# A pair loop of expert blocks in which part of the up split goes to GpSimd and the sums of halves and rows come first

## The chip, the cores and the metric

The kernel runs on one core of one Trainium2 chip. The metric is the device time of one execution in microseconds, lower being better. Engines: TensorE (PE in the profile), VectorE (DVE), ScalarE (ACT), GpSimd (POOL) and SyncE (SP), which here only starts transfers.

## The reference, cut to what matters

Two transformer blocks on 256 tokens of width 1024, in fp32. The first has three kinds of attention, the second a convolution with sparse attention and then a mixture of experts. Only the experts matter for this change. Each token goes to 8 of 64 experts, each with hidden width 256:

```python
def expert_block(args):
    e, toks, gs = args
    xb = t[toks]
    return swiglu(xb, w1[e], w3[e], w2[e]) * gs[:, None]     # (silu(x @ w1) * (x @ w3)) @ w2
routed = segment_sum(out, row_tok)                            # rows back to their tokens, summed
```

The weights of one expert are 1 MB each for w1, w3 and w2.

## The kernel before

Up to about 650 us the kernel computes the first block and the attention of the second. Then a loop runs over a list of expert blocks; a block is one expert with up to 128 of its tokens. Its length is a run-time value. The blocks alternate. Even ones are "whole": room for 128 tokens. Odd ones are "half": room for 64 tokens. The loop's bodies are written out for BODY = 4 blocks.

Precision comes from splits. Every operand x is held as x_hi = round(x) in a fast fp32 form, written by ScalarE, and x_lo = x - x_hi, written by VectorE. A product is the sum of passes hi*hi, hi*lo and lo*hi. A whole block makes 24 matmuls of 128x512 in its up product (8 steps k, three passes). A half block puts x_hi in the lower 64 columns of the stationary operand and x_lo in the upper 64, makes 16 matmuls, and then adds the two halves of the result ("sum of halves": ScalarE copies the lower half to `hsum`, VectorE adds the other half to it).

The up weights of a block (w1 as m = 0, w3 as m = 1) are split in four pieces of 128x1024, named (kh, m): kh is the half of the steps k (k 0 to 3 or 4 to 7). A matmul of step k reads both m. The down weights are split in two pieces. The up weights of block i + 1 are split while block i is worked on, its down weights in its own body.

The order within block i on each engine is written out by hand; semaphores carry the dependences.

- TensorE (`expert_block`, L2110): up product (L2124) into `hidden_b`; transposes of the rows of block i + 1 into `y_b` (`turn_rows`, L2083 to L2096); the scatter of block i - 1, which adds y into `acc_b` by means of the 0/1 matrix `put` (L2104, in two halves; the second one gives `block_done`); transposes of h (L2144) into `turned_b`; the token search of block i + 2 (`find_tokens`, L2079, into columns of `hidden_b`); the down product (L2162) into `y_b`. In a whole block the second half of the scatter stands behind the transposes of h.
- ScalarE: two roundings of down weights (L1173); two of the four up roundings of block i + 1 (L1156, pieces of kh 0); in a half block the copy of the lower half (L1183); silu (L1189); the rounding of the rows (`round_rows`, L1146 and L1151); h_hi (L1192); the other two up roundings; y_hi (L1200) twice.
- VectorE (`expert_block`, L1695): two subtractions of down weights (L1702); two of up weights (L1676); in a half block the sum of halves (L1708); h = silu * up (L1711); the low part of the rows (`rest_of_rows`, L1664 and L1670); the low part of h (L1715); `take_tokens` (L1656 to L1658), which copies what the token search found; two more up subtractions; y_lo (L1725) twice.
- GpSimd: `make_pick` for block i + 2 (L901, a 0/1 matrix for the token search); after `block_done` of this body the matrix `put` for block i (L931); the indirect transfer `gather_rows` for block i + 2 (L912).
- SyncE: for block i, once down_lo of block i - 2 is made, the transfers of w1, w3 and w2 into the raw buffer that it used, and then small columns for block i + 2.

## Time and profile before

| | us |
|---|---|
| median of 3 runs (1066.08 to 1070.39) | 1069.08 |
| the profiled execution | 1068.22 |
| its span in the trace | 1066.3 |
| TensorE matmuls busy | 980.1 (92%) |
| VectorE busy | 783.9 (74%) |
| ScalarE busy | 584.1 (55%) |
| GpSimd busy | 284.4 (27%) |

Busy times are over the whole span. The expert loop fills roughly the last 400 us, and there the shares differ. Matmuls are pipelined: one takes 0.40 us from start to end, and the next starts 0.23 us after it. "Idle before" in a row is the time in which the engine stood before that instruction, and the arrow names what ended it.

### The profile page before, as it was taken

The page shows a single profiled execution, that of the slowest core. Times are in us where ns is not written, and L with a number is a line of the kernel's source. Part 1 is how long each engine was busy: PE and PEld are TensorE (multiplying, and loading weights), DVE is VectorE, ACT ScalarE, POOL GpSimd, SP SyncE. Part 2 cuts the span into 40 slices and gives each one's busy share as a digit, 9 for nine tenths or more (in the row PEclk, how much of TensorE's full clock was granted, in tenths as well). Part 3 has the DMA queues.
Part 4 walks back from the last instruction along what each step waited for, and adds up shares of the span by engine and source line. Part 5 has one row for each costly group of instructions (what it writes and reads, how often), then busy time and mean ns, then how long its engine had stood idle before and what let it go on. Part 6 is the DMA issues. An engine that isn't in the chain of part 4 may idle for free. (4 is left out here: it accounts for less than half of the span.)

```text
span 1066.3 us, 16044 instructions
## 1 busy us (share of the span) xinstructions
PE 980.1 (92%) x4988; PEld 777.4 (73%) x4988; DVE 783.9 (74%) x1351; ACT 584.1 (55%) x894; POOL 284.4 (27%) x357
## 2 busy tenths in 40 slices
PE   8999999999999999989879989899898989999886
PEld 7877877788766676778768876677676777777664
DVE  4677888678843543567775655889989889898987
ACT  4554565435533242435426424777767777777774
POOL 5154442224100000031226113233222322232221
PEclk9999999999999899999989999999999999999998
DMA  9877767759624243436242317788778877887773
GB/s 308 275 257 256 248 227 252 251 183 309 213 90 150 89 158 119 169 95 234 80 158 80 112 55 267 288 313 318 285 279 317 317 276 271 310 315 290 285 308 143
DMA packets 79285, 238.54 MB, mean 224 GB/s; under 512 B 12732, under 2 KB 18933, under 8 KB 65922
## 3 DMA queue, kind: packets, MB, share of 16 engines
q1 hardware_dynamic: 66002, 196.60, 50.4%
q0 software_dynamic: 12656, 40.87, 11.4%
q8 instruction: 29, 0.48, 0.2%
q10 hardware_dynamic: 576, 0.41, 0.1%
q14 instruction: 22, 0.18, 0.1%
HBM read 235.55 MB, written 2.16 MB: 223 GB/s over the span
## 5 line engine op out<-in xcount | busy, mean ns | idle before, releaser
L1846 PE MATMUL bank<-w_hi,a_hi 128*128 128x512 f32 (+2 forms) x512 | 205.8, 402 | 8.6 <-POOL w_lo L857 3.8
L1846 PE MATMUL bank<-w_hi,a_lo 128*128 128x512 f32 (+2 forms) x512 | 196.8, 384 | 0.0
L1846 PE MATMUL bank<-w_lo,a_hi 128*128 128x512 f32 (+2 forms) x512 | 196.4, 384 | 0.0
L1281 DVE TENSOR_TENSOR w_lo<-ring,w_hi 128x1024 fp32r<-128x1024 f32 (+2 forms) x132 | 152.9, 1181 | 53.2 <-ACT w_hi L991 48.6
L991 ACT ACTIVATE w_hi<-ring 128x1024 fp32r<-128x1024 f32 (+2 forms) x140 | 141.0, 1023 | 73.8 <-PE bank L1846 70.1
L1676 DVE TENSOR_TENSOR up_lo<-raw_weights,up_hi 128x1024 fp32r<-128x1024 f32 x136 | 161.2, 1227 | 1.0 <-ACT up_hi L1156 0.5
L1156 ACT ACTIVATE up_hi<-raw_weights 128x1024 fp32r<-128x1024 f32 x136 | 135.6, 1048 | 1.3 <-DMA raw_weights<-in_w_dram 1.3
L1846 PEld LDWEIGHTS bank<-w_hi,a_hi 128*128 128x128 f32 x512 | 96.5, 188 | 38.4 <-issue 16.6
L1846 PEld LDWEIGHTS bank<-w_hi,a_lo 128*128 128x128 f32 x512 | 96.4, 188 | 19.8
L1846 PEld LDWEIGHTS bank<-w_lo,a_hi 128*128 128x128 f32 x512 | 96.7, 189 | 18.3 <-issue 1.4
L2124 PE MATMUL bank<-up_hi,x_block_hi 128*128 128x512 f32 x264 | 104.4, 395 | 1.0 <-issue 1.0
L2124 PE MATMUL bank<-up_lo,x_block_hi 128*128 128x512 f32 x264 | 104.4, 396 | 0.0
L931 POOL TENSOR_SCALAR put<-slots,block_tokens_f 128x256 fp32r<-128x256 f32 x33 | 30.5, 924 | 233.0 <-issue 233.0
L818 POOL DMA_DIRECT2D merged<-in_w_ada_dram x96 | 53.2, 556 | 127.5 <-DVE ada_acc L1420 93.9
L798 POOL TENSOR_SCALAR mean_squares<-mean_squares 128x8 f32<-128x8 f32 (+2 forms) x32 | 9.9, 310 | 283.9 <-ACT logits L944 204.1
L1702 DVE TENSOR_TENSOR down_lo<-raw_weights,down_hi 128x1024 fp32r<-128x1024 f32 x66 | 77.9, 1222 | 7.5 <-ACT down_hi L1173 7.4
L2162 PE MATMUL bank<-down_hi,h_hi 128*128 128x512 f32 x132 | 58.9, 446 | 18.0 <-DVE h_hi L1715 17.4
L1173 ACT ACTIVATE down_hi<-raw_weights 128x1024 fp32r<-128x1024 f32 x66 | 66.0, 1051 | 0.3 <-issue 0.3
L1420 DVE SCALAR_TENSOR_TENSOR ada_acc<-merged,c_col,ada_acc 128x512 f32<-128x512 f32 x84 | 62.7, 747 | 4.2 <-DMA merged<-in_w_ada_dram 1.0
L1200 ACT ACTIVATE y_hi<-bank,block_gates 128x512 fp32r<-128x512 f32 x66 | 45.4, 689 | 32.8 <-PE bank L2162 32.1
L2124 PEld LDWEIGHTS bank<-up_hi,x_block_hi 128*128 128x128 f32 x264 | 50.0, 189 | 13.2 <-issue 1.2
L2124 PEld LDWEIGHTS bank<-up_lo,x_block_hi 128*128 128x128 f32 x264 | 49.6, 188 | 12.1
(281 smaller groups left out, 1874.3 us busy)
## 6 DMA issues: line engine op xcount, KB each, us to landing
raw_weights<-in_w_dram SPq DMA_DIRECT2D x102, 1024.0 KB, 6.9
ring<-in_w_in_dram SPq DMA_DIRECT2D x58, 1024.0 KB, 5.9
merged<-in_w_ada_dram POOLq DMA_DIRECT2D x96, 256.0 KB, 4.4
ring<-in_w_out_dram SPq DMA_DIRECT2D x8, 1024.0 KB, 5.8
ring<-in_w_branch_dram SPq DMA_DIRECT2D x6, 1024.0 KB, 4.8
bias<-rel_rows SPq DMA_DIRECT2D x40, 128.0 KB, 4.9
ring<-in_ws_dram SPq DMA_DIRECT2D x2, 1024.0 KB, 5.1
merged<-in_x_dram SPq DMA_DIRECT2D x2, 512.0 KB, 5.7
```

The source lines that it names most:

```text
L818: gp.dma_start(ada_row(q), src).then_inc(S(f"ada_loaded_{q % ADA_SLOTS}"), 16)
L991: act.activation(w_parts[0][:, 2 * p:2 * p + 2, 0:w], view(j, kind)[:, 2 * p:2 * p + 2, :], ACT.Copy)\
L1156: act.activation(up_hi[:, r % 2, 4 * kh:4 * kh + 4, m, :], raw_up(raw[:, 1 - r % 2, :], kh, m), ACT.Copy)\
L1173: act.activation(down_hi[:, f, :], raw[:, 1 - r % 2][:, UP + f * DM:UP + (f + 1) * DM], ACT.Copy)\
L1200: act.activation(y_hi[:, hf * CH:(hf + 1) * CH], y_b[hf][:, :], ACT.Copy, scale=gcol[:, r, 0:1])\
L1281: dve.tensor_tensor(w_parts[1][:, 2 * p:2 * p + 2, 0:w], view(JOB[it[1:3]], kind)[:, 2 * p:2 * p + 2, :], w_parts[0][:, 2 * p:2 * p + 2, 0 ...
L1420: dve.scalar_tensor_tensor(out=o, in0=ada_row(q), scalar=c_col[:, 1, k:k + 1], in1=o, op0=ALU.mult, op1=ALU.add) .then_inc(S("ada_step" if ...
L1676: dve.tensor_tensor(up_lo[:, r % 2, 4 * kh:4 * kh + 4, m, :], raw_up(raw[:, 1 - r % 2, :], kh, m), up_hi[:, r % 2, 4 * kh:4 * kh + 4, m, : ...
L1702: dve.tensor_tensor(down_lo[:, f, :], raw[:, 1 - r % 2][:, UP + f * DM:UP + (f + 1) * DM], down_hi[:, f, :].bitcast(F32), ALU.subtract).th ...
L1846: mm = pe.matmul(ps[:, 0:wide], a_parts[za][:, k, t * P:(t + 1) * P], w_parts[zw][:, k, 0:wide], start=start, stop=stop)
L2124: mm = pe.matmul(hidden_b[:, :], (xe_hi, xe_lo)[zx][:, k, :], (up_hi, up_lo)[zw][:, r % 2, k].rearrange("p m n -> p (m n)"), start=(k == 0 ...
L2162: mm = pe.matmul(y_b[hf][:, :], (h_hi, h_lo)[zh][:, f, :], (down_hi, down_lo)[zw][:, f, hf * CH:hf * CH + CH], start=(n == 0), stop=(n == ...
```

## The change

What moves, and where it goes:

- The token search of block i + 2 stands at the head of TensorE's block, before the up product, and writes to four columns of `turned_b` (`found_b`). VectorE copies its result at the head of its own block.
- In a half block ScalarE makes no up roundings before the copy of the lower half; the rows of the next block are rounded between that copy and the silu; all four up roundings stand behind h_hi. VectorE does the sum of halves right after the down subtractions, then one half of the rows, then h, then the other half of the rows, the low part of h, and then three up subtractions.
- In a whole block VectorE does one up subtraction before h and two behind the low part of h; ScalarE's order stays.
- One of the four up subtractions goes to GpSimd: (0, 1) where the next block is half, (1, 1) where it is whole. GpSimd does it last in its block, behind `put`. TensorE waits for it at k = 0 of a half block, at k = 4 of a whole one.
- GpSimd starts the gather of block i + 2 first in its block, and makes the pick of block i + 3 second.
- SyncE loads the up weights of block i once the up split of block i - 2 is done (VectorE's three pieces and GpSimd's one), and the down weights once down_lo of block i - 2 is done.

```diff
@@ sync
-                        sp.wait_ge(S("down_lo"), 2 * i - 2)
-                        load_down(r, load_up(i, r))
+                        sp.wait_ge(S("up_lo"), 3 * i - 3)
+                        sp.wait_ge(S("up_lo_pool"), i - 1)
+                        e = load_up(i, r)
+                        sp.wait_ge(S("down_lo"), 2 * i - 2)
+                        load_down(r, e)
                         load_columns(i + 2, (r + 2) % BODY)
@@ gpsimd
+            def rest_of_up_weights(i, r):
+                kh = 0 if r % 2 else 1
+                gp.wait_ge(S("up_hi"), 4 * i + 2 * kh + 2)
+                gp.sem_inc(S("begun"), 1)
+                gp.tensor_tensor(up_lo[:, r % 2, 4 * kh:4 * kh + 4, 1, :], raw_up(raw[:, 1 - r % 2, :], kh, 1),
+                                 up_hi[:, r % 2, 4 * kh:4 * kh + 4, 1, :].bitcast(F32), ALU.subtract).then_inc(S("up_lo_pool"), 1)
+
             for i in range(2):
                 make_pick(i, i, 1)
                 gather_rows(i, i, 0)
+            make_pick(2, 2, 1)
+            rest_of_up_weights(0, 0)
...
-                        after = (r + 2) % BODY
-                        make_pick(i + 2, after, m4 + 1 + (r + 2) // BODY)
-                        gp.wait_ge(S("slots_loaded"), 16)
+                        gather_rows(i + 2, (r + 2) % BODY, m4 * (BODY // 2) + (r + 2) // 2)
+                        make_pick(i + 3, (r + 3) % BODY, m4 + 1 + (r + 3) // BODY)
                         gp.wait_ge(S("block_done"), i + 1)
                         gp.tensor_scalar(put[:, :], slots[:, S_TOK:S_TOK + TOK], tok_f[:, r, 0:1], None, ALU.is_equal)\
                           .then_inc(S("put_ready"), 1)
-                        gather_rows(i + 2, after, m4 * (BODY // 2) + (r + 2) // 2)
+                        rest_of_up_weights(i + 1, (r + 1) % BODY)
@@ scalar
                         nxt = (r + 1) % BODY
-                        act.wait_ge(S(f"up_loaded_{nxt}"), 32 * (m4 + 1 + (r + 1) // BODY))
-                        for m in range(2):
-                            round_up_weights(nxt, 0, m)
                         if r % 2:
                             act.wait_ge(S("up_done"), i + 1)
                             act.activation(hsum[0:HALF, :], hidden_b[HALF:P, :], ACT.Copy).then_inc(S("half_low_copied"), 1)
+                            round_rows(nxt, m4 * (BODY // 2) + (r + 1) // 2)
                             act.wait_ge(S("half_summed"), m4 * (BODY // 2) + (r // 2 + 1))
+                            act.activation(hs[0:HALF, 0, :], hsum[0:HALF, 0:ED], ACT.Silu).then_inc(S("silu_done"), 1)
                         else:
+                            act.wait_ge(S(f"up_loaded_{nxt}"), 32 * (m4 + 1 + (r + 1) // BODY))
+                            for m in range(2):
+                                round_up_weights(nxt, 0, m)
...
+                        if r % 2:
+                            act.wait_ge(S(f"up_loaded_{nxt}"), 32 * (m4 + 1 + (r + 1) // BODY))
+                            for m in range(2):
+                                round_up_weights(nxt, 0, m)
                         for m in range(2):
                             round_up_weights(nxt, 1, m)
@@ vector
+                take_tokens(i + 2, (r + 2) % BODY, found_b)
                 for f in range(FT):
                     ...down_lo...
-                for m in range(2):
-                    rest_of_up_weights(i + 1, nxt, 0, m)
                 if half:
                     ...sum of halves...
+                    rest_of_whole_rows(pair(1), 0)
+                    ...h...
+                    rest_of_whole_rows(pair(1), 1)
+                    ...low part of h...
+                    for kh, m in UP_OF_EVEN:                      # (0, 0), (0, 1), (1, 0)
+                        rest_of_up_weights(i + 1, nxt, kh, m)
+                else:
+                    rest_of_up_weights(i + 1, nxt, 0, 0)
+                    ...h, rows, low part of h...
+                    for m in range(2):
+                        rest_of_up_weights(i + 1, nxt, 1, m)
@@ tensor
                 pe.wait_ge(S("tokens_ready"), i + 2)
+                find_tokens(i + 2, (r + 2) % BODY, found_b)
                 for k in range(KT):
                     if k % 4 == 0:
-                        pe.wait_ge(S("up_lo"), 4 * i + k // 2 + 2)
+                        pe.wait_ge(S("up_lo"), 3 * i + k // 4 * 2 + 1 if half else 3 * i + k // 4 + 2)
+                    if k == (0 if half else 4):
+                        pe.wait_ge(S("up_lo_pool"), i + 1)
...
-                find_tokens(i + 2, (r + 2) % BODY)
```

## Rows read from the trace of the kernel before

**Rows 1.** The page's costliest groups: the matrix put, one for each block.

```profile
L931 POOL TENSOR_SCALAR put<-slots,block_tokens_f 128x256 fp32r<-128x256 f32 x33 | 30.5, 924 | 233.0 <-issue 233.0
```

**Rows 2.** Busy time of each engine in one pair of blocks.

```profile
core 0: us, PE busy (x) PEld busy (x) DVE busy (x) ACT busy (x) POOL busy (x), PEclk, DMA share, GB/s
815.73:839.23 23.50, 21.08 (x102) 16.53 (x100) 21.27 (x32) 17.81 (x24) 6.98 (x9) 1.00 0.79 303
```

**Rows 3.** Waits from 700 to 1050 us: total, times, longest.

```profile
PE bank L2162 <- DVE h_hi L1715: 16.3, 15, 1.1
...
PE bank L2096 <- DMA x_gathered<-h_rows,block_tokens: 14.2, 15, 1.4
```

**Rows 4.** TensorE's timeline, 815 to 840 us: start, length, line, [idle before].

```profile
815.73 0.40 PE L2124 MATMUL bank<-up_hi,x_block_hi 128*128 128x512 f32 x1
...
819.23 0.40 PE L2124 MATMUL bank<-up_lo,x_block_hi 128*128 128x512 f32 x1
820.61 1.09 PE L2096 MATMUL bank<-consts,x_gathered 128*128 128x128 f32 x8 [0.98 <-DMA x_gathered<-h_rows,block_tokens]
...
823.18 0.40 PE L2104 MATMUL bank<-y_lo,put 128*128 128x512 f32 x1
...
825.75 0.49 PE L2162 MATMUL bank<-down_hi,h_hi 128*128 128x512 f32 x1 [1.14 <-DVE h_hi L1715]
...
827.70 0.39 PE L2124 MATMUL bank<-up_hi,x_block_hi 128*128 128x512 f32 x1
...
833.07 0.40 PE L2124 MATMUL bank<-up_hi,x_block_lo 128*128 128x512 f32 x1
...
836.37 0.48 PE L2162 MATMUL bank<-down_hi,h_hi 128*128 128x512 f32 x1
...
839.23 0.40 PE L2124 MATMUL bank<-up_hi,x_block_hi 128*128 128x512 f32 x1
```

**Rows 5.** ScalarE's timeline in the same pair.

```profile
820.43 0.59 ACT L1183 ACTIVATE hidden_sum<-bank 64x512 f32<-64x512 f32 x1
822.86 0.42 ACT L1189 ACTIVATE hs<-hidden_sum 64x256 f32<-64x256 f32 x1 [1.84 <-DVE hidden_sum L1708]
823.30 1.08 ACT L1151 ACTIVATE x_block_hi<-bank 128x512 fp32r<-128x512 f32 x2
824.33 0.28 ACT L1192 ACTIVATE h_hi<-bank 128x128 fp32r<-128x128 f32 x1
824.50 2.00 ACT L1156 ACTIVATE up_hi<-raw_weights 128x1024 fp32r<-128x1024 f32 x2
...
833.50 0.39 ACT L1189 ACTIVATE hs<-bank 128x256 f32<-128x256 f32 x1 [1.12 <-PE bank L2124]
...
835.77 2.00 ACT L1156 ACTIVATE up_hi<-raw_weights 128x1024 fp32r<-128x1024 f32 x2
```

**Rows 6.** VectorE's timeline in the same pair.

```profile
822.15 0.68 DVE L1708 TENSOR_TENSOR hidden_sum<-bank,hidden_sum 64x512 f32<-64x512 f32 x1
...
825.59 2.36 DVE L1676 TENSOR_TENSOR up_lo<-raw_weights,up_hi 128x1024 fp32r<-128x1024 f32 x2
```

**Rows 7.** GpSimd's timeline in the same pair, whole block.

```profile
836.59 0.93 POOL L931 TENSOR_SCALAR put<-slots,block_tokens_f 128x256 fp32r<-128x256 f32 x1 [7.57 <-issue]
```

**Rows 8.** GpSimd's subtraction in the attention: ns min/median/max, first and last start.

```profile
L857 POOL TENSOR_TENSOR w_lo<-ring,w_hi x8: 2377/2410/3056, 454.0 to 597.1; 128x1024 fp32r<-128x1024 f32 x8
```

**Rows 9.** GpSimd and VectorE from 526 to 542 us; the VectorE line's times.

```profile
529.18 9.64 POOL L857 TENSOR_TENSOR w_lo<-ring,w_hi 128x1024 fp32r<-128x1024 f32 x4 [6.07 <-ACT w_hi L991]
...
531.67 2.37 DVE L1576 TENSOR_TENSOR selmask<-score,consts 128x128 f32<-128x128 f32 x1
...
L1576 DVE TENSOR_TENSOR selmask<-score,consts x2: 427/1400/2374, 531.7 to 544.8; 128x128 f32<-128x128 f32 x1, 128x256 f32<-128x256 f32 x1
```

**Rows 10.** GpSimd and VectorE from 674 to 678 us; the times of pick.

```profile
674.88 3.06 POOL L901 TENSOR_SCALAR pick<-slots,block_cols 128x128 fp32r<-128x128 f32 x2
675.20 2.36 DVE L1702 TENSOR_TENSOR down_lo<-raw_weights,down_hi 128x1024 fp32r<-128x1024 f32 x2 [0.37 <-ACT down_hi L1173]
...
L901 POOL TENSOR_SCALAR pick<-slots,block_cols x70: 602/630/2460, 647.2 to 1042.9; 128x128 fp32r<-128x128 f32 x70
```

More of the change, by code:

```diff
@@ L403 @@
 HALF = P // 2
-UP_PIECES = ((0, 0), (0, 1), (1, 0), (1, 1))
+UP_OF_EVEN = ((0, 0), (0, 1), (1, 0))
 MAX_WORK = N_EXP + TOK * 8 // (P + 1)
@@ L767, in _ @@
                     else:
+                        sp.wait_ge(S("up_lo"), 3 * (r - 1))
+                        sp.wait_ge(S("up_lo_pool"), r - 1)
+                        e = load_up(r, r)
                         sp.wait_ge(S("down_lo"), 2 * (r - 1))
-                        e = load_up(r, r)
                     load_down(r, e)
@@ L1176, in _ @@
                         nxt = (r + 1) % BODY
-                        act.wait_ge(S(f"up_loaded_{nxt}"), 32 * (m4 + 1 + (r + 1) // BODY))
-                        for m in range(2):
-                            round_up_weights(nxt, 0, m)
-                        rows = HALF if r % 2 else P
                         if r % 2:
@@ L1686, in _ @@
             shared_h(0)
-            take_tokens(0, 0)
+            take_tokens(0, 0, hidden_b)
             shared_h(1)
-            take_tokens(1, 1)
-            for kh, m in UP_PIECES:
+            take_tokens(1, 1, hidden_b)
+            for kh, m in UP_OF_EVEN:
                 rest_of_up_weights(0, 0, kh, m)
-            rest_of_rows(0, 0)
+            for q in range(2):
+                rest_of_whole_rows(0, q)
             dve.wait_ge(S("work_ready"), 3)
@@ L1698, in expert_block @@
                 half = r % 2
-                rows = HALF if half else P
+                take_tokens(i + 2, (r + 2) % BODY, found_b)
                 for f in range(FT):
@@ L1709, in expert_block @@
                        .then_inc(S("half_summed"), 1)
-                dve.wait_ge(S("silu_done"), i + 1)
-                dve.tensor_tensor(he[0:rows], hs[0:rows, 0, :], (hsum if half else hidden_b)[0:rows, ED:2 * ED], ALU.mult)\
-                   .then_inc(S("h_done"), 1)
-                rest_of_rows(nxt, pair(1))
-                dve.wait_ge(S("h_hi_ready"), i + 1)
-                dve.tensor_tensor(h_hi[:, :, HALF:P] if half else h_lo[:, :, :],
-                                  turned_b[:, 0:FT * rows].rearrange("p (f n) -> p f n", f=FT),
-                                  h_hi[:, :, 0:rows].bitcast(F32), ALU.subtract).then_inc(S("h_lo_ready"), 1)
-                take_tokens(i + 2, (r + 2) % BODY)
-                for m in range(2):
-                    rest_of_up_weights(i + 1, nxt, 1, m)
+                    rest_of_whole_rows(pair(1), 0)
+                    dve.wait_ge(S("silu_done"), i + 1)
+                    dve.tensor_tensor(he[0:HALF], hs[0:HALF, 0, :], hsum[0:HALF, ED:2 * ED], ALU.mult).then_inc(S("h_done"), 1)
+                    rest_of_whole_rows(pair(1), 1)
+                    dve.wait_ge(S("h_hi_ready"), i + 1)
+                    dve.tensor_tensor(h_hi[:, :, HALF:P], turned_b[:, 0:FT * HALF].rearrange("p (f n) -> p f n", f=FT),
+                                      h_hi[:, :, 0:HALF].bitcast(F32), ALU.subtract).then_inc(S("h_lo_ready"), 1)
+                    for kh, m in UP_OF_EVEN:
+                        rest_of_up_weights(i + 1, nxt, kh, m)
+                else:
+                    rest_of_up_weights(i + 1, nxt, 0, 0)
+                    dve.wait_ge(S("silu_done"), i + 1)
+                    dve.tensor_tensor(he, hs[:, 0, :], hidden_b[:, ED:2 * ED], ALU.mult).then_inc(S("h_done"), 1)
+                    rest_of_half_rows(pair(1))
+                    dve.wait_ge(S("h_hi_ready"), i + 1)
+                    dve.tensor_tensor(h_lo[:, :, :], turned_b[:, 0:FT * P].rearrange("p (f n) -> p f n", f=FT),
+                                      h_hi[:, :, :].bitcast(F32), ALU.subtract).then_inc(S("h_lo_ready"), 1)
+                    for m in range(2):
+                        rest_of_up_weights(i + 1, nxt, 1, m)
                 for hf in range(2):
@@ L2074, in _, with find_tokens @@
               .then_inc(S("list_product"), 1)
-            def find_tokens(i, r):
+            def find_tokens(i, r, found):
                 pe.wait_ge(S("pick_ready"), NT * i + NT)
                 for t in range(NT):
-                    mm = pe.matmul(hidden_b[:, 0:4], pick[:, r % 2, t, :], col4[:, r, 4 * t:4 * t + 4],
+                    mm = pe.matmul(found, pick[:, r % 2, t, :], col4[:, r, 4 * t:4 * t + 4],
                                    start=(t == 0), stop=(t == 1))
```

40 lines of the change are left out of this document (19 added, 21 removed).

## The prediction

> **What bounds the kernel now.** I read first the page's groups and the waits to find where TensorE is held, then the timelines of one pair of expert blocks, engine by engine, then Pool's rows from elsewhere in the program, because the change gives Pool a kind of work that its loop did not have. The loop handles 33 blocks [rows 1]; they alternate, 17 whole (even numbers) and 16 half (odd). One pair lasts 23.50 us at full clock, with TensorE's matmuls busy 21.08 us of it and VectorE 21.27 [rows 2]. So two engines are nearly full, and TensorE stands in two places, both after the up product of the half block: about 1 us for the gathered rows of the next block, and about 1.1 us for the low part of h [rows 3]. From 700 to 1050 us each came 15 times. If both vanished and nothing came instead, a pair would gain some 2 us, 16 pairs some 33 us.
>
> In the pair that I follow [rows 4], the half block's up product runs from 815.73 to 819.46 (the last start plus the pitch of 0.233, which is 3.50 us over 15 starts). I call that end A. The whole block's up product ends at 833.30; I call that B. The next half block's up product starts at 839.23. So A to B is 13.84, B to the next start is 5.93, and the up product itself 3.73: 23.50 in all. I rebuild the two stretches with the new order. All times below are counted from A or from B.
>
> **Stretch A to B (half block's h, its down product, the whole block's up product).** Before, ScalarE's copy of the lower half began at 0.97, since it was behind two roundings of up weights, VectorE's sum at 2.69, behind two up subtractions, and TensorE's transposes of rows at 1.15 [rows 4 to 6]. Now the roundings and subtractions are behind. ScalarE follows a finished product by 0.20 (833.30 to 833.50 [rows 5]). So: copy 0.21 to 0.80; sum (0.68) 0.84 to 1.52. The gather now starts a whole block earlier, right after the token search, so I count it as landed: transposes and scatter, 2.80 from 820.61 to 823.41, run from 0.10 to 2.90. ScalarE rounds the rows (1.08) from 0.80 to 1.88 and then does the silu; silu start to h_hi start was 1.47 (822.86 to 824.33), so h_hi runs from 3.35 to 3.63. VectorE's two row subtractions are now on both sides of the product with silu and end before 3.5. The low part of h takes 0.28 (3.66 to 3.94, an estimate from h_hi's own length on ScalarE), and TensorE follows by about 0.3: down product at 4.27, against 6.29 before. That is 2.0 us won.
>
> Most of it is given back. The four up roundings of the whole block now all stand behind h_hi: two took 2.00 with starts 0.95 apart, and the first began 0.17 after h_hi's start [rows 5]. They end at 4.56, 5.51, 6.46 and 7.41. VectorE's subtractions (two take 2.36, starts 1.14 apart [rows 6]) end at 5.82, 6.96 and 8.10. The down product (1.95, 825.75 to 827.70) ends at 6.22, but the first up matmul wants both pieces of kh 0: 6.96 plus a handover, 7.2. The two matmuls of the token search, now ahead of the up product, lie in that wait and cost nothing; without it they would cost some 0.3. Twelve matmuls (2.80) bring TensorE to k = 4 at 10.0. There it needs Pool's piece (1,1). Pool's subtraction of this very shape takes 2.41 in the stage before [rows 8]; started at 7.45 it would end at 9.86, just in time. But VectorE's last up piece runs until 8.02, and I let Pool's begin when that is over (reason below): 7.95 to 10.36, up product on at 10.5, end 13.3. So A to B goes from 13.84 to 13.3: **minus 0.54**, or minus 1.04 where Pool's piece is not held.
>
> ScalarE's y_hi comes two roundings later (7.4), VectorE's y_lo with it; TensorE needs them only after B, so this is covered, with over 3 us to spare.
>
> **Stretch B to the next half block's up product.** Here the order of TensorE is as before, since the half block's sum isn't in it; one token search moves from before the down product to behind it. The new thing is Pool's queue. In this block Pool does the gather and the picks first (both long before B), then waits for block_done, which TensorE gives after the second scatter, then does put, and only then the piece (0,1) of the next half block. Its first matmul, k = 0, waits for that piece. Put began at B + 3.29 and took 0.93 [rows 7]: it ends at 4.22. The piece is 2.41: 6.66 at the earliest, up product at 6.8, against 5.93. TensorE's cover for it, the down product of 2.86 (836.37 to 839.23), is too short by 0.87 in each pair, with no contention at all. The roundings that the piece needs were done before B; nothing else holds it.
>
> Contention comes on top. VectorE reads two SBUF operands in up_lo and down_lo. Where Pool's four subtractions ran back to back from 529.18, a VectorE subtraction of 128x128 took 2.37, while the same line took 0.427 for twice the elements, its shortest [rows 9]: it waited out Pool's piece. The other way: a pair of picks begun at 674.88 took 3.06 in place of twice 0.63, and ended at 677.94, after both down subtractions of VectorE (675.20 to 677.56), which were not slowed [rows 10]. So each of the two waits for the whole of the other, and Pool missed the gap between two VectorE instructions that followed each other. In the new loop Pool asks at 4.27. VectorE's piece (1,0) starts when ScalarE's rounding is done (835.77 plus 1.0 [rows 5]: 3.57), the next (1,1) at 4.71, back to back, end 5.85. By the rows of the picks Pool misses the gap at 4.71 and begins at about 5.8: end 8.2, up product at **8.35, plus 2.42**. If Pool gets in at 4.63, it ends at 7.04, up product at 7.2 (plus 1.27), and (1,1) is held until 8.2, which puts y_lo, the token copies and down_lo back until the sum of halves is some 0.4 late: plus 1.67.
>
> The Trainium skill speaks to this in "SBUF — State Buffer", section "Who interferes with whom": a VectorE instruction with two SBUF inputs contends with a GpSimd instruction that reads SBUF, whoever issues first holds the port for its whole instruction, and issue order decides who blocks. The trace agrees on the whole instruction (2.37 against 0.427); on who comes first the picks disagree, as the second of them began before the second down subtraction and still lost. By the skill's rule the sum would be the one with plus 1.67.
>
> **Edits at no cost.** The loads of up weights are issued earlier, after up_lo and the Pool piece of two blocks before; that leaves over 10 us before their rounding, and what is queued behind them on SP, the down load and the columns, waits anyway for down_lo in the block that follows, which is later than both new waits. On Pool the gather is moved ahead of the picks, of the wait for block_done and of put; it waits for the tokens alone. Token copies stand at the head of VectorE's block, 0.3 in a stretch that waits for down_hi anyway. In the prologue VectorE has one piece less and Pool one more, before the first up product, which waits for gathered rows; uncovered it would be at most one piece, 2.4 us once.
>
> **The sum.** 16 stretches A to B at minus 0.54 are minus 8.6. The first transition has no scatter before it, so 15 at plus 2.42 are plus 36.3. Together plus 27.7 on the profiled execution's 1068.2, so 1095.9; it stood 0.9 below the median of the runs, so I say 1096.
>
> **The rivals.**
> 1. Pool gets the gap (first come, first served): 15 times 1.67 minus 8.6 is plus 16.5, so 1085. For it: put keeps a mean of 924 ns over all 33 blocks [rows 1], though up subtractions stand near it. Against it: the pick that lost.
> 2. Pool and VectorE do not hold each other in the loop: minus 1.04 times 16, plus 0.87 times 15, is minus 3.6, 1065: no change. Against it: the two kinds of row that show each engine held [rows 9, 10].
> 3. The other side: the up pieces reach TensorE in time, so that A to B is bare work: 4.27 + 1.95 + 0.2 + 5.6 = 12.0, minus 1.8 in each of 16, and without contention plus 13 on the other stretch: minus 16, 1053. It decides from the point where A to B falls below 12.7. Against it: four roundings behind h_hi, which no row shows faster than 0.95 apart.
> 4. Contention in both stretches (Pool's piece (1,1) also missing a gap, or picks holding down_lo and the sum of halves): another 0.5 to 1 us per pair, 1104 to 1112.
>
> **How the numbers follow.** Forecast 0.42, rival 1 0.25, rival 2 0.15, rival 3 0.08, rival 4 0.10. The forecast's own range is 1090 to 1103. A measurement of this kernel tells about 0.5% from no change, 1064 to 1074. The range 1068 to 1106 leaves out rival 3, half of rival 2 and part of rival 4. Faster 0.08 (rival 3), within 0.5% 0.15 (rival 2), slower 0.77.
>
> **What the profile after would show.** Right: no wait for gathered rows; ScalarE's copy of the half at A + 0.2; down product of the half block near A + 4.3; a TensorE wait for up_lo of VectorE of 0.7 to 1 before the whole block's up product; a TensorE wait of 2 us or more before each half block's up product, released by Pool; that Pool piece beginning before 5 us after B but lasting well over 2.41. A pair of about 25.4. Wrong: Pool's piece at 2.4 there with VectorE's pieces at 1.22 (rival 2), or VectorE's piece (1,1) at 3 us and more (rival 1). If put doesn't have to wait for the second scatter, the whole second stretch is wrong.

## The result, and the profile after

The changed kernel takes 1072.93 us (median of 5, 1072.43 to 1073.65), the kernel before 1066.17 us (median of 5, 1066.03 to 1070.39). The ratio is 1.0051, with a 95% interval of 1.0031 to 1.0071: slower by half a per cent (the ratio is that of the means, 1067.5 and 1073.0; the medians lie 6.8 us apart). The forecast was 1096, a loss of 28 us; the loss is about 5 us. The profiled execution has a span of 1070.6 us, against 1066.3 before.

The pair of blocks answers to the one of [rows 2]. Busy time of each engine in it:

```profile
core 0: us, PE busy (x) PEld busy (x) DVE busy (x) ACT busy (x) POOL busy (x), PEclk, DMA share, GB/s
816.58:840.84 24.26, 21.30 (x100) 16.54 (x100) 21.55 (x29) 17.50 (x25) 14.07 (x10) 1.00 0.79 293
```

A pair is 24.26 us, 0.76 longer than the 23.50 of before, where I had said 25.4. The timeline of TensorE shows in which places it stands (answers to [rows 4]):

```profile
start us, us, engine line op out<-in xcount [idle before <-releaser]
816.58 0.50 PE L2153 MATMUL bank<-up_hi,x_block_hi 128*128 128x512 f32 x1 [1.15 <-POOL up_lo L927]
...
820.17 0.39 PE L2153 MATMUL bank<-up_lo,x_block_hi 128*128 128x512 f32 x1
820.40 1.03 PE L2122 MATMUL bank<-consts,x_gathered 128*128 128x128 f32 x8
...
824.61 0.49 PE L2190 MATMUL bank<-down_hi,h_hi 128*128 128x512 f32 x1 [0.92 <-DVE h_hi L1733]
...
827.39 0.50 PE L2153 MATMUL bank<-up_hi,x_block_hi 128*128 128x512 f32 x1 [0.55 <-DVE up_lo L1695]
...
830.80 0.50 PE L2153 MATMUL bank<-up_hi,x_block_hi 128*128 128x512 f32 x1 [0.35 <-POOL up_lo L927]
...
833.47 0.40 PE L2153 MATMUL bank<-up_hi,x_block_lo 128*128 128x512 f32 x1
...
840.84 0.50 PE L2153 MATMUL bank<-up_hi,x_block_hi 128*128 128x512 f32 x1 [1.14 <-POOL up_lo L927]
```

A, the end of the half block's up product, is 820.40; B is 833.47 plus the pitch of 0.233, 833.70. The wait for gathered rows before the transposes [rows 3] is gone: these follow at A at once. Instead of two stands there are four: 0.92 for h, 0.55 and 0.35 for pieces of the whole block's up weights, and 1.14 for GpSimd's piece ahead of the half block. A to B is 13.30, B to the next start 7.14, the up product 3.82.

The waits from 700 to 1050 us (total, times, longest) say that this is in every pair; they answer to [rows 3]:

```profile
PE bank L2153 <- POOL up_lo L927: 21.2, 29, 1.2
...
PE bank L2190 <- DVE h_hi L1733: 13.9, 15, 0.9
...
PE bank L2153 <- DVE up_lo L1695: 8.3, 15, 0.6
```

GpSimd's and VectorE's timelines show the disputed place, here 7.2 us after B of the pair ahead (B is 809.43 there):

```profile
812.74 0.93 POOL L946 TENSOR_SCALAR put<-slots,block_tokens_f 128x256 fp32r<-128x256 f32 x1 [1.91 <-PE bank L2130]
813.63 2.89 POOL L927 TENSOR_TENSOR up_lo<-raw_weights,up_hi 128x1024 fp32r<-128x1024 f32 x1
...
813.00 4.60 DVE L1695 TENSOR_TENSOR up_lo<-raw_weights,up_hi 128x1024 fp32r<-128x1024 f32 x2 [0.52 <-ACT up_hi L1171]
...
814.21 3.39 DVE L1695 TENSOR_TENSOR up_lo<-raw_weights,up_hi 128x1024 fp32r<-128x1024 f32 x1
```

The last row is the second of the two that make up the row above it, from a narrower stretch. VectorE's first piece runs from 813.00. GpSimd comes at 813.63 and is done at 816.52; less its own 2.41 [rows 8] its work began at 814.11, within 0.2 of the end of VectorE's first piece (VectorE's second starts at 814.21). VectorE's second piece lasts 3.39 where it has 1.2 of work: it waited for GpSimd to end. So GpSimd did get the gap that I said it would miss. TensorE goes on 0.06 after it.

**Where the 4.3 us of span come from.** Up to the start of the second whole block the changed kernel is 3.65 us ahead (681.73 against 685.38), of which 3.27 are there when the loop starts (659.07 against 662.34), in code that the change leaves nearly alone (kernels of this study that are alike up to there start the loop anywhere from 659.1 to 662.3, so I count it as no effect of the change). The next fifteen pairs take 364.12 (to 1045.85) against 358.32 (to 1043.70): 5.80 lost. What follows takes 24.75 against 22.60: 2.15 lost. The sum is 4.30. Fifteen pairs at 0.76 would be 11.4, not 5.8, because before's pairs are not all like the one that I followed: their mean is 23.89, not 23.50. In four of them, at 777, 849, 968 and 1040 us, TensorE's clock falls. The timeline and a stretch of before show the first:

```profile
777.24 0.76 PE L2162 MATMUL bank<-down_hi,h_hi 128*128 128x512 f32 x1 [1.10 <-DVE h_hi L1715]
...
778.22 0.63 PE L2162 MATMUL bank<-down_hi,h_hi 128*128 128x512 f32 x1
778.65 0.63 PE L2162 MATMUL bank<-down_lo,h_hi 128*128 128x512 f32 x1
...
777.00:781.00 4.00, 3.76 (x10) 2.96 (x11) 3.23 (x6) 1.76 (x4) 2.50 (x3) 0.57 1.01 426
```

The matmuls there start 0.43 apart, not 0.233, and the granted clock of the stretch is 0.57: the engine is at 1.2 GHz in most of it. TensorE had stood 0.97, 0.31 and 1.10 us within the six us before. Each of these falls costs some 1.5 us (the whole block starts 13.4 to 13.5 us after the half, not 11.93). The changed kernel has none in its loop. Before, then the changed kernel, over most of the loop:

```profile
700.00:1040.00 340.00, 303.97 (x1424) 237.86 (x1422) 303.80 (x431) 254.51 (x345) 98.77 (x113) 0.98 0.77 297
...
700.00:1040.00 340.00, 298.45 (x1403) 231.58 (x1402) 301.95 (x393) 245.38 (x337) 197.19 (x141) 1.00 0.79 292
```

So about 5.8 us of the loss were given back by something that the prediction had no term for. The stands alone don't decide when the clock falls: before has about the same three in each of the fifteen pairs, the one of [rows 4] among them (0.98, 0.30, 1.14, clock 1.00), and it fell in four. It differs from run to run as well: of 17 runs of before, one with a mean clock of 0.988 spanned 1062.4 us and one with 0.972 spanned 1076.4. That the changed kernel escapes because its stands lie further apart is argued, not tested.

The tail costs 2.15: the last up product 0.72 (it waits for GpSimd's piece in its middle), and 1.43 at the very end. There GpSimd makes a piece for a block that doesn't come, it holds VectorE, y_lo is late, and the last scatter runs after the stand at the slow clock:

```profile
1061.13 0.75 PE L2130 MATMUL bank<-y_hi,put 128*128 128x512 f32 x1 [3.10 <-DVE y_lo L1751]
...
1061.00:1065.00 4.00, 3.66 (x8) 2.49 (x8) 2.45 (x4) 0.00 (x0) 0.00 (x0) 0.57 0.00 0
```

### The profile page after: what moved, and what is told of

It reads as the page before. It is cut to its first block and busy times, and to the rows that moved or that the text cites. A ratio compares the mean times of both kernels' runs of the same rounds, so it can differ in the third digit from the quotient of the medians.

```text
span 1070.6 us, 16195 instructions
## 1 busy us (share of the span) xinstructions
PE 976.4 (91%) x4988; PEld 771.3 (72%) x4988; DVE 787.5 (74%) x1317; ACT 579.3 (54%) x894; POOL 402.4 (38%) x393
## 5 line engine op out<-in xcount | busy, mean ns | idle before, releaser
L1695 DVE TENSOR_TENSOR up_lo<-raw_weights,up_hi 128x1024 fp32r<-128x1024 f32 x102 | 158.1, 1591 | 19.5 <-ACT up_hi L1171 19.4
L2153 PE MATMUL bank<-up_hi,x_block_hi 128*128 128x512 f32 x264 | 109.6, 415 | 32.4 <-POOL up_lo L927 22.7
L927 POOL TENSOR_TENSOR up_lo<-raw_weights,up_hi 128x1024 fp32r<-128x1024 f32 x34 | 95.6, 2812 | 57.0 <-ACT up_hi L1171 57.0
L1722 DVE TENSOR_TENSOR down_lo<-raw_weights,down_hi 128x1024 fp32r<-128x1024 f32 x66 | 88.6, 1381 | 0.1
L918 POOL DMA_INDIRECT x_gathered<-h_rows,block_tokens x35 | 50.7, 1448 | 67.5 <-DVE block_tokens_f L1677 48.7
L907 POOL TENSOR_SCALAR pick<-slots,block_cols 128x128 fp32r<-128x128 f32 x72 | 64.4, 900 | 22.5 <-DMA block_cols<-pcol 20.2
L2190 PE MATMUL bank<-down_hi,h_hi 128*128 128x512 f32 x132 | 53.6, 406 | 15.5 <-DVE h_hi L1733 14.8
```

What stands on the lines that cost most here:

```text
L907: gp.tensor_scalar(pick[:, r % 2, t, :], slots[:, at:at + P], col4[:, r, 4 * t + 3:4 * t + 4].bitcast(F32), None, ALU.is_equal)\
L927: gp.tensor_tensor(up_lo[:, r % 2, 4 * kh:4 * kh + 4, 1, :], raw_up(raw[:, 1 - r % 2, :], kh, 1), up_hi[:, r % 2, 4 * kh:4 * kh + 4, 1, :] ...
L1695: dve.tensor_tensor(up_lo[:, r % 2, 4 * kh:4 * kh + 4, m, :], raw_up(raw[:, 1 - r % 2, :], kh, m), up_hi[:, r % 2, 4 * kh:4 * kh + 4, m, : ...
L1722: dve.tensor_tensor(down_lo[:, f, :], raw[:, 1 - r % 2][:, UP + f * DM:UP + (f + 1) * DM], down_hi[:, f, :].bitcast(F32), ALU.subtract).th ...
L2153: mm = pe.matmul(hidden_b[:, :], (xe_hi, xe_lo)[zx][:, k, :], (up_hi, up_lo)[zw][:, r % 2, k].rearrange("p m n -> p (m n)"), start=(k == 0 ...
```

## The experiments

Ratios are to the kernel before, in the same runs (its median there 1066.7 to 1067.9).

**1. The change without GpSimd's piece.** All four subtractions on VectorE, one before h in a whole block and three behind it.

```diff
-            rest_of_up_weights(0, 0)                      # gpsimd, and at the end of its block
-                        rest_of_up_weights(i + 1, (r + 1) % BODY)
-UP_OF_EVEN = ((0, 0), (0, 1), (1, 0))
+UP_OF_EVEN = ((0, 0), (0, 1), (1, 0), (1, 1))
-                    for m in range(2):                     # vector, whole block, behind h
-                        rest_of_up_weights(i + 1, nxt, 1, m)
+                    for kh, m in UP_OF_EVEN[1:]:
+                        rest_of_up_weights(i + 1, nxt, kh, m)
```

> The changed kernel, with all four up subtractions on VectorE: behind the low part of h in a half block; one before h and three behind it in a whole block. GpSimd has none. Theory 1 (the Pool piece behind put is what costs: 1.15 us of TensorE's wait before each half block, and 0.35 before k = 4 of a whole one): both waits go, VectorE has 2.3 us more per pair and becomes the fullest engine; pair 23.0 to 23.4 against 24.26 of the changed kernel and 23.5 before; 16 pairs, so 1055 to 1062. Rival (the move of up roundings behind h_hi costs, not the Pool piece): the pair stays near 24.0 to 24.3 and the time near 1070.

Measured: 1044.17 us (1043.66 to 1046.23), ratio 0.978 [0.975, 0.981]. A pair, and what is left of TensorE's waits in it:

```profile
808.49:831.01 22.52, 21.04 (x104) 16.46 (x102) 20.98 (x31) 17.51 (x24) 10.68 (x9) 1.00 0.86 315
```
```profile
816.51 0.49 PE L2184 MATMUL bank<-down_hi,h_hi 128*128 128x512 f32 x1 [0.92 <-DVE h_hi L1729]
819.29 0.50 PE L2147 MATMUL bank<-up_hi,x_block_hi 128*128 128x512 f32 x1 [0.56 <-DVE up_lo L1691]
```

VectorE's busy time falls from 21.55 to 20.98 although it does one piece more in each block (its length counts the time in which it is held: 2.2 us in the 3.39 piece above, 0.7 in down_lo beside GpSimd's other piece). The rest of the change is worth 2.2%; GpSimd's piece costs 28.8 us, 1.74 in each pair. The gain is larger than I expected (1055 to 1062).

**2. GpSimd's piece ahead of the scatter.** In whole blocks alone GpSimd does it before it waits for block_done.

```diff
+                        if r % 2 == 0:
+                            rest_of_up_weights(i + 1, (r + 1) % BODY)
                         gp.wait_ge(S("block_done"), i + 1)
                         gp.tensor_scalar(put[:, :], ...)
-                        rest_of_up_weights(i + 1, (r + 1) % BODY)
+                        if r % 2:
+                            rest_of_up_weights(i + 1, (r + 1) % BODY)
```

> The changed kernel; in whole blocks alone GpSimd makes its up piece before it waits for block_done and makes put. Theory 1 (GpSimd's piece is late because it stands behind the wait for block_done and put): the piece is done about 3.9 us after the end of the whole block's up product, TensorE's wait of 1.15 before the half block goes, pair 22.9 to 23.1, time about 1052 to 1056. Rival (the shared port): GpSimd holds VectorE's subtractions or is held by them wherever the piece stands, so that only part comes back: pair 23.5 or more, 1062 or more.

Measured: 1051.71 us (1048.84 to 1052.46), ratio 0.984 [0.981, 0.987]; a pair is 22.97, as forecast. The stand of 1.14 is gone, those of 0.56 and 0.35 stay. One move of one instruction is worth 1.29 a pair, 21 us: it was the place in GpSimd's queue that cost most, not the work. GpSimd's timeline, and VectorE's beside it, hold a surprise:

```profile
805.77 2.39 POOL L927 TENSOR_TENSOR up_lo<-raw_weights,up_hi 128x1024 fp32r<-128x1024 f32 x1
808.14 2.94 POOL L948 TENSOR_SCALAR put<-slots,block_tokens_f 128x256 fp32r<-128x256 f32 x1
...
807.96 2.42 DVE L1698 TENSOR_TENSOR up_lo<-raw_weights,up_hi 128x1024 fp32r<-128x1024 f32 x2 [0.53 <-ACT up_hi L1174]
```

Now put lasts 2.94 in place of 0.93, and VectorE's two pieces take their bare 2.42. It came 0.18 after the first of the two and ended at 811.08, 0.7 after the second. That is the picks' behaviour [rows 10]: this instruction misses the gap that GpSimd's subtraction gets. It does so in each of the 16 whole blocks behind the first (2.94 each time).

**3. The same, with one rounding earlier.** In half blocks ScalarE also rounds piece (0, 0) before it waits for the end of the up product, where it stands otherwise (2.67 us in the changed kernel, before its copy).

```diff
                         if r % 2:
+                            act.wait_ge(S(f"up_loaded_{nxt}"), 32 * (m4 + 1 + (r + 1) // BODY))
+                            round_up_weights(nxt, 0, 0)
                             act.wait_ge(S("up_done"), i + 1)
...
-                            for m in range(2):
-                                round_up_weights(nxt, 0, m)
+                            round_up_weights(nxt, 0, 1)
```

> The kernel piece_before_put, and in half blocks ScalarE makes the first of the four up roundings (piece 0, 0) before it waits for the end of the up product, where the changed kernel has it idle for 2.67 us. Theory: the rounding ends before the copy of the lower half is due, so the waits for up_lo (0.55) and for GpSimd's piece at k = 4 (0.35) shrink by about 0.6 together; pair 22.3 to 22.6, time 1045 to 1050. Rival: with TensorE's wait before the half block gone, ScalarE has no slack there any more and the copy comes late by up to 0.5: pair as in piece_before_put or longer.

Measured: 1038.99 us (1038.07 to 1040.51), ratio 0.973 [0.970, 0.975]; a pair is 22.21. Both are under what I had forecast. The wait of 0.56 for VectorE's pieces is gone; 0.31 at k = 4 for GpSimd's stays. So the wait that A to B got in the changed kernel came from four roundings in a row behind h_hi, as the prediction's working has it.

**4. GpSimd only writes.** Its subtraction is replaced by two memsets of the same piece; the low part of that piece is left out of the computation.

```diff
-                gp.tensor_tensor(up_lo[...piece...], raw_up(...), up_hi[...piece...], ALU.subtract)
+                gp.memset(up_lo[...piece...], 0.0)         # twice
```

> The changed kernel with GpSimd's up subtraction replaced by two fills of the same piece with zeros, so the low part of that piece of the up weights is left out of the product. It reads nothing from SBUF. Theory (GpSimd's reads hold VectorE's second operand and the other way round): in whole blocks the VectorE subtraction that took 3.5 us next to GpSimd's piece takes 1.2, the fills start at once behind put, and down_lo is not lengthened from 2.35 to 3.05 for two. Rival (any GpSimd instruction that touches SBUF does it): VectorE's subtractions stay lengthened while a fill runs.

Measured: 1047.87 us (one run); a pair is 22.82. GpSimd and VectorE side by side:

```profile
805.36 0.96 POOL L927 MEMSET up_lo<- 128x1024 f32 x1
...
804.75 2.43 DVE L1697 TENSOR_TENSOR up_lo<-raw_weights,up_hi 128x1024 fp32r<-128x1024 f32 x2 [0.52 <-ACT up_hi L1173]
```

Neither holds the other: VectorE's two pieces take 2.43 with a memset in the middle. It is GpSimd's reading that collides. The time can't be used as the price of the collision, since two memsets (2.06 with their gap) are shorter than the subtraction (2.41).

**5. put with a constant.** Experiment 2, with the token column replaced by the number 5.0, so that put, and with it the scatter, has other contents.

```diff
-                        gp.tensor_scalar(put[:, :], slots[...], tok_f[:, r, 0:1], None, ALU.is_equal)
+                        gp.tensor_scalar(put[:, :], slots[...], 5.0, None, ALU.is_equal)
```

> The kernel piece_before_put, with put compared with the constant 5.0 in place of each row's token number, so that the scatter adds rows to wrong tokens; all shapes and the order stay. In piece_before_put, put began 0.2 us after the first of two back-to-back up subtractions and took 2.94 in place of 0.92: it missed the gap between them. GpSimd's own subtraction in the changed kernel, in the same place, got that gap. Theory: an instruction with a scalar from SBUF has to get at SBUF twice, once for the scalar and once for its tensor, and so waits for two gaps; with a constant, put waits for one: about 1.8 us. Rival (chance or queue order decides who gets the gap): 2.9 as before.

Measured: 1052.68 us (one run), and in the place that matters:

```profile
808.45 1.71 POOL L948 TENSOR_SCALAR put<-slots 128x256 fp32r<-128x256 f32 x1
...
808.17 2.62 DVE L1698 TENSOR_TENSOR up_lo<-raw_weights,up_hi 128x1024 fp32r<-128x1024 f32 x2 [0.52 <-ACT up_hi L1174]
```

2.94 becomes 1.71 (1.70 to 1.71 in all 17 whole blocks). VectorE's first piece starts at 808.17 and takes 1.28, to 809.45; put ends at 810.16, 0.71 after it, so it had the first gap. In experiment 2, with the column, it ended 0.7 after the second piece, so it had the second. Experiment 1 shows the second gap once more, with three pieces in a row:

```profile
806.02 2.71 POOL L943 TENSOR_SCALAR put<-slots,block_tokens_f 128x256 fp32r<-128x256 f32 x1
...
805.60 3.76 DVE L1691 TENSOR_TENSOR up_lo<-raw_weights,up_hi 128x1024 fp32r<-128x1024 f32 x3
807.95 1.41 DVE L1691 TENSOR_TENSOR up_lo<-raw_weights,up_hi 128x1024 fp32r<-128x1024 f32 x1
```

The last row is the third piece alone. put came 0.42 after the first, and ended at 808.73, 0.71 after the end of the second (808.02). The reading that fits is that this instruction reads SBUF twice, first its column of scalars and then the rows, and waits each time for VectorE's running instruction. That it waits twice is shown; what it reads first is my reading.

**6. The token search alone.** The kernel before, with search, token copies, gather and pick moved as in the change, and nothing else.

```diff
+                find_tokens(i + 2, (r + 2) % BODY, found_b)        # tensor, head of the block
+                take_tokens(i + 2, (r + 2) % BODY, found_b)        # vector, head of the block
+                        gather_rows(i + 2, ...)                    # gpsimd, first
+                        make_pick(i + 3, ...)
```

> The kernel before with one part of the change: token search, token copies, picks and gather moved as in the changed kernel, everything else in the old order, four up subtractions on VectorE. Theory: the wait of 1 us for gathered rows in each pair goes, but the sum of halves still stands behind two up subtractions on VectorE (2.7 us after the product), so TensorE meets that wait 1 us earlier and little is gained: pair 23.3 to 23.5, 1060 to 1068 by the pairs. The four stretches at half clock of before come after the two waits in a row; with one of them gone they should be gone too, which would be another minus 6. Rival: the gather wait was the path: pair 22.5, 1050.

Measured: 1086.80 us (1084.27 to 1091.69), ratio 1.020 [1.016, 1.024]: slower, and the clock moved against what I had expected. The wait for rows is gone, but TensorE's waits behind it grow, and they now stand close to each other:

```profile
808.00 0.42 PE L2144 MATMUL bank<-consts,hT 64*128 64x64 f32 x2 [1.59 <-DVE hT L1711]
...
809.54 0.79 PE L2161 MATMUL bank<-down_hi,h_hi 128*128 128x512 f32 x1 [1.11 <-DVE h_hi L1715]
...
810.56 0.63 PE L2161 MATMUL bank<-down_hi,h_hi 128*128 128x512 f32 x1
...
809.00:813.00 4.00, 3.46 (x10) 2.76 (x10) 3.19 (x5) 2.32 (x3) 0.00 (x0) 0.57 1.01 428
700.00:1040.00 340.00, 298.62 (x1346) 236.12 (x1345) 291.64 (x407) 243.33 (x327) 122.17 (x109) 0.92 0.77 281
```

After 1.59 and 1.11 of standing the clock is granted at 0.57, over and over: its mean from 700 to 1040 us is 0.92, where before has 0.98. Of 15 pairs four keep the full clock; they take 23.48 to 23.86, no less than before's, since the sum of halves is as late as ever. The other 11 take 24.9 to 26.6. The shortest of the four has stands of 1.50 and 1.19, about as long as the others', so here too the stands alone don't decide it.

**7. The order in the half block alone.** The kernel before, with sums and rows first and the roundings behind h_hi as in experiment 1, but search, gather, pick and SyncE's loads where they were. (The whole block also has one piece ahead of h and three behind it, as in experiment 1.)

```diff
                         if r % 2:
                             ...copy of the lower half...
+                            round_rows(nxt, ...)
                             ...silu...
+                            for m in range(2):                     # scalar, behind h_hi
+                                round_up_weights(nxt, 0, m)
+                    rest_of_whole_rows(pair(1), 0)                 # vector, half block
+                    ...h, rows, low part of h...
+                    for kh, m in UP_OF_EVEN:                       # all four
+                        rest_of_up_weights(i + 1, nxt, kh, m)
```

> The kernel before with the other part of the change: sums of halves and rows first on ScalarE and VectorE, the up roundings of half blocks behind h_hi, as in four_on_vector (four pieces on VectorE); token search, picks, gather and loads stay as before. Theory: TensorE still waits some 1 us for gathered rows, ScalarE's row roundings and the silu behind them come 1 us later than in four_on_vector, so a pair is 23.3 to 23.5 where the clock is full, against 22.5 with both parts; and since the wait for h is short now, TensorE doesn't stand twice within a few us and falls to half clock seldom or never: 1058 to 1064. Rival (this order brings the gain alone): 1046 to 1050.

Measured: 1097.53 us (1097.17 to 1099.80), ratio 1.029 [1.027, 1.031]: slower by more than any other, and again not what I expected. TensorE, then ScalarE, in one half block, and the wait over 700 to 1050 us:

```profile
806.85 1.09 PE L2108 MATMUL bank<-consts,x_gathered 128*128 128x128 f32 x8 [2.33 <-DMA x_gathered<-h_rows,block_tokens]
...
807.54 1.09 ACT L1151 ACTIVATE x_block_hi<-bank 128x512 fp32r<-128x512 f32 x2 [2.39 <-PE bank L2108]
...
PE bank L2108 <- DMA x_gathered<-h_rows,block_tokens: 33.9, 14, 3.4
```

The rows are late (33.9 us over 14 waits, against 14.2 over 15 in [rows 3]), and silu, h_hi and all four up roundings are queued behind them: ScalarE's rounding of rows is now ahead of the silu, and TensorE transposes h after the rows, as it did before. A pair at full clock takes 24.9 to 25.0, against 23.45 for most of before's. In one of them (A at 830.58) the transposes of rows start at A + 2.54 (before 1.15), the down product at 6.82 (6.29) and the up product at 9.60 (8.24). So the late rows cost 1.4, the early sum wins back 0.9, and the roundings behind h_hi cost 0.8; the stretch from the whole block to the half is 0.2 longer too. On top of it the clock falls in seven of fifteen pairs (26.2 to 27.6 us), where I had expected seldom or never; its mean from 700 to 1040 us is 0.96.

Why are the rows late? SyncE's loads of weights and the gather, here and in before:

```profile
821.88 0.82 SPq L747 DMA_DIRECT2D raw_weights<-in_w_dram  x2
825.33 1.31 POOL L912 DMA_INDIRECT x_gathered<-h_rows,block_tokens  x1 [0.20 <-issue]
...
809.31 0.82 SPq L747 DMA_DIRECT2D raw_weights<-in_w_dram  x2
814.22 1.31 POOL L912 DMA_INDIRECT x_gathered<-h_rows,block_tokens  x1 [0.20 <-issue]
```

The gather starts 5.2 before A in both (A is 830.58 and 819.46). The loads, which wait for down_lo of the whole block, start 8.70 before A here and 10.15 in before, since VectorE makes four up pieces between the low part of h and that down_lo, in before two; and the rows land 1.4 later. Loads that run 1.4 later beside the gather would explain it; no run tests that.

**8. The token search with the gap filled.** Experiment 6 with eight matmuls of 128x252 in each half block, ahead of the transposes of h, whose results nobody reads.

```diff
+                if half:
+                    pe.wait_ge(S("down_lo"), 2*i+2)
+                    for n in range(8):
+                        pe.matmul(turned_b[:, 260:512], down_hi[:, 0, 0:P], down_hi[:, 0, 0:252], start=True, stop=True)
```

> The kernel search_first_only with eight matmuls of 128x252 more in each half block, between the second scatter and the transposes of h, where TensorE stood 1.5 us for the sum of halves; their results go to unused columns and are not read. Theory (the half clock in 10 of the 16 pairs comes from TensorE standing 1.5 and 1.1 us with next to nothing in between): TensorE stands less, the half-clock stretches go, every pair is 23.5, and the time is 1062 to 1066 in place of 1086.8. Rival (the half clock has another cause, as the transfers or the whole load of the chip): 1085 to 1090.

Measured: 1072.24 us (1065.39 to 1075.82), ratio 1.003 [1.000, 1.006]. The stretch from 700 to 1040 us:

```profile
700.00:1040.00 340.00, 311.41 (x1532) 252.01 (x1531) 301.67 (x424) 253.23 (x339) 123.21 (x112) 0.98 0.80 294
```

Useless work on TensorE makes experiment 6 faster by 14.6 us, and the mean clock is back at 0.98. So most of what experiment 6 lost is the clock and not the stands themselves. A few slow stretches remain, and the time is 6 us above the 1066 that was the upper end of what I expected. Of the 20 us that experiment 6 lost against the kernel before, 6 are left.

**9. The best of it.** Experiments 1 and 3 together: no piece on GpSimd, one rounding before the up product's end.

> The kernel four_on_vector (no piece on GpSimd), and in half blocks ScalarE makes the first up rounding before it waits for the end of the up product. Theory: four_on_vector still has a TensorE wait of 0.55 for up_lo before each whole block, and that one goes; there is no wait at k = 4; pair 21.9 to 22.0 against 22.51, 1034 to 1036, faster than the best so far (1039). Rival: VectorE, busy 21.3 of 22.5 us in a pair, is the bound and lets at most 0.3 through: 1039 to 1044.

Measured: 1032.88 us (1030.64 to 1035.32), ratio 0.968 [0.965, 0.971].

```profile
801.76:823.53 21.77, 20.85 (x104) 16.38 (x102) 20.89 (x31) 17.53 (x24) 10.70 (x9) 1.00 0.87 326
```

It beats both kernels, and is a little under what I had forecast (1034 to 1036). Of the pair's 21.77 us, TensorE stands once, 0.92 for the low part of h. It is 6 us better than experiment 3, which has GpSimd's piece: even well placed, the piece costs more than it frees.

## Why the prediction went wrong, by its steps

**Stretch A to B: right in every step, to within 0.2 us.** Copy at A + 0.19 (said 0.21); sum of halves at A + 0.91 (0.84); h_hi at A + 3.32 (3.35); down product at A + 4.21 (4.27); up product at A + 6.99 (7.2); k = 4 at A + 10.40 (10.5); end at 13.30 (13.3). ScalarE's and VectorE's timelines show the head of it (answers to [rows 5, 6]):

```profile
820.59 0.59 ACT L1194 ACTIVATE hidden_sum<-bank 64x512 f32<-64x512 f32 x1 [2.67 <-PE bank L2153]
...
823.72 0.28 ACT L1207 ACTIVATE h_hi<-bank 128x128 fp32r<-128x128 f32 x1 [1.13 <-PE bank L2173]
823.89 3.89 ACT L1171 ACTIVATE up_hi<-raw_weights 128x1024 fp32r<-128x1024 f32 x4
...
821.31 0.67 DVE L1726 TENSOR_TENSOR hidden_sum<-bank,hidden_sum 64x512 f32<-64x512 f32 x1
```

The four roundings in one row are those that give back what the early sum won.

**Stretch B to the next start: the step that failed.** It is "By the rows of the picks Pool misses the gap at 4.71 and begins at about 5.8: end 8.2, up product at 8.35, plus 2.42". Everything up to it held: GpSimd asks at B + 4.20 (said 4.27), VectorE's pieces start at 3.57 (3.57) and 4.78 (4.71). But GpSimd's subtraction began at about 4.68 and ended at 7.09, and the up product started at 7.15, plus 1.22. That is rival 1's mechanism. The step was priced at 2.42 a pair and is 1.22: over 15 pairs 18.0 of the 23.4 us by which forecast (27.7) and measured span (4.3) differ. I had put the picks [rows 10] above the rule of the Trainium skill in "SBUF — State Buffer", section "Who interferes with whom", that issue order decides; here the trace agrees with the rule for the two subtractions (813.63 before 814.21, and GpSimd went first). For put and the picks it doesn't: put came at 808.14, before VectorE's second piece, and ended 0.7 after that piece. Experiment 5 shows what is different: an operand of scalars in SBUF costs a second wait. The rows that I took were of another kind of instruction than the one that I priced, and that is why they misled. A row of the right kind was in the trace of before, behind [rows 9]: VectorE's subtraction came at 531.67, GpSimd's second piece ran from 531.52 to 533.90 and its third followed at 533.87; VectorE was done at 534.04, so it had got the gap between two pieces that followed each other.

**Rival 1 had the mechanism and not the time.** It said 1085. The measured 1072.93 is inside the stated 1068 to 1106, and nearer to rival 2's 1065, but that is luck: the clock (5.8) and the earlier start of the loop (3.3), which neither rival had, took 9 us off. Only the rows tell the rivals apart.

**Rival 1's 0.4 of lateness: not there.** VectorE's piece is held until B + 8.17 (said 8.2), and y_lo, token copies and down_lo are late with it, but the sum of halves starts at A + 0.91, only 0.07 after what I had for it undisturbed. B's next start had moved as well: a shift of the whole chain doesn't count twice. With 1.22 in place of 2.42, 15 stretches are 18.3 and not 36.3.

**The baseline: one pair stood for all.** I summed against an undisturbed pair of 23.50. Before's pairs have a mean of 23.89, and the reason, the falls of the clock, is absent from the changed kernel's. By the steps as measured, 16 times minus 0.54, 15 times 1.22 and 1.4 for up products (3.82, as they now start after a stand, against 3.73) are 11; the clock gives 5.8 of it back; the tail takes 2.1. That is 7.4 us; less the earlier start of the loop, 3.3, which the change doesn't explain, 4.1 of the span's 4.3. The row was there to be read: over 700 to 1050 us the fastest pair and the mean pair differ.

**The other items.** No wait for gathered rows: right, in all pairs. The wait of VectorE's up_lo was 0.55, a little below the 0.7 to 1 that I gave. A wait of 2 us or more before the half block: wrong, 1.14. The Pool piece there lasts 2.89, "well over 2.41", though for another reason than I had (0.48 of waiting, not a missed gap). VectorE's piece at 3 us and more was the sign that I had named for rival 1, and it is there: 3.39. Rival 2 (no holding) falls by that row. Rival 3 falls by the two waits of A to B. But experiment 9 shows that it was possible: only the place of one rounding stood in its way, and the piece on GpSimd.

**What the parts are worth.** Search alone plus 20 us, order in the half block alone plus 31, both together minus 24 (experiments 6, 7 and 1). They are not a sum, and a third part is in neither 6 nor 7: SyncE's loads, which in the changed kernel and in experiment 1 wait for up_lo and no longer for down_lo. What that part is worth by itself is not measured. Each alone shortens one of two stands and makes the other worse: the early search leaves the sum of halves late, and the waits for h come close together and cost the clock; the early sum puts silu and roundings behind rows that come later than before (a median of 7.0 us from the gather's issue, 6.0 before). That the slow clock explains most of experiment 6 is shown by experiment 8; the terms of experiment 7 are read from its trace, and none of them is tested by itself.

## What to carry to other kernels

When an instruction is handed to a second engine, read what that engine's queue waits for ahead of it: moving the same subtraction ahead of one wait was worth 21 us of 1073, and not moving it to GpSimd at all 29. When parts of a change are tested alone, list every wait that each part moves: here the loads belonged to neither. When a row is used to price contention, it must be of the same kind of instruction, operands included. And take the mean of all passes of a loop as the baseline, not a clean one: if they differ, what makes the others longer is itself a thing that the change can remove or bring.

## What the runs showed of the hardware

- On GpSimd a subtraction of two SBUF tensors begins when VectorE's running two-operand subtraction ends, even if the next one follows at once (2.89 us: 0.48 of waiting, 2.41 of work). A tensor_scalar with a column of scalars in SBUF lets one more go by: put takes 0.92 us with nothing in its way, 2.94 and 2.71 when it comes during a row of VectorE subtractions (experiments 2 and 1). With a constant it is 0.85 and 1.71.
- A memset on GpSimd (0.96 us for 128x1024) neither holds nor is held by VectorE's subtraction (two in 2.43 us).
- TensorE's clock fell to 1.2 GHz after stands of which none was longer than 1.6 us (0.97, 0.31 and 1.10 before; 1.59 and 1.11 in experiment 6), with a granted clock of 0.57 over the 4 us after. Such stands didn't always bring it down: before has about the same in fifteen pairs, and the clock fell in four. The changed kernel, whose stands are 0.92, 0.55, 0.35 and 1.14 us over a pair of 24 us, had a granted clock of 1.00 from 700 to 1040 us. Putting useless matmuls into one of experiment 6's stands gave back 14.6 us.
